# Meta columns and tokens in one operand: matmul passes of 264, 264 and 512 columns instead of 16, 512 and 512

## The reference

```python
meta = jnp.broadcast_to(meta_tokens.astype(x.dtype)[None], (B, N_META, D_MODEL))   # N_META = 16
h = jnp.concatenate([meta, x], axis=1)
L = h.shape[1]                                                                      # 1040
...
xn = rms_norm_2(h, norm_mix_g[layer])
proj = jnp.einsum('bld,de->ble', xn, w_in[layer])
q, k, v, f_logit, b_gate, c_gate, u = jnp.split(proj, split_at, axis=-1)
log_f = jax.nn.log_sigmoid(f_logit.astype(jnp.float32) + b_f[layer].astype(jnp.float32))
...
y_attn = forgetting_attention(q.reshape(hs), k.reshape(hs), v.reshape(hs), log_f)
y_conv = b_gate * causal_depthwise_conv(c_gate * u, conv_w[layer].astype(u.dtype))
```

## Time and profile before

| | |
|---|---|
| Median of 3 runs | 2525.3 us (2525.23 to 2527.97) |
| Profiled execution | 2522.91 us, span 2521.0 us |
| Mean granted clock of PE | 0.919 |
| PE busy | 2194.3 us (87%), 9596 matmuls |
| DVE busy | 1117.7 us (44%) |
| POOL busy | 498.1 us (20%) |
| ACT busy | 413.5 us (16%) |
| Chain that ended last | PE 71%, DVE 23%, ACT 2% |
| of it, line 594 | 60% |

### The profile page before, as it was taken

How to read it: one execution, slowest core, us unless ns; L and a number is a source line. 1 busy time by engine, 2 the same in 40 slices (tenths; PEclk the granted TensorE clock), 3 DMA queues, 4 the chain that set the end, 5 groups by cost and what they waited for, 6 DMA issues and landing times.

```text
span 2521.0 us, 23118 instructions
## 1 busy us (share of the span) xinstructions
PE 2194.3 (87%) x9596; PEld 1734.7 (69%) x9596; DVE 1117.7 (44%) x1222; ACT 413.5 (16%) x591; POOL 498.1 (20%) x375
## 2 busy tenths in 40 slices
PE   6999989797878229789999868799899999999997
PEld 5787778576666117568787644457788888888886
DVE  4143542769999973451452134541422221222123
ACT  3001441310110032120010033330320011011001
POOL 2232002122211001111322120002222222222221
PEclk8999889799889659799999879999899999999998
DMA  4223002122222002132224132232223333323332
GB/s 147 83 92 100 1 19 92 48 77 75 67 71 71 17 0 76 58 114 77 76 77 127 36 68 60 60 97 92 75 92 93 99 93 98 100 92 100 93 100 100
DMA packets 53443, 196.23 MB, mean 78 GB/s; under 512 B 6993, under 2 KB 7249, under 8 KB 52865
## 3 DMA queue, kind: packets, MB, share of 16 engines
q1 hardware_dynamic: 30144, 113.56, 14.5%
q0 software_dynamic: 22320, 81.27, 10.8%
q10 hardware_dynamic: 912, 0.51, 0.1%
HBM read 172.02 MB, written 8.46 MB: 72 GB/s over the span
## 4 chain that ended last, share of the span: by engine, by line
PE 71%; DVE 23%; ACT 2%; issue 2%; DMA 1%; POOL 1%; SPq 0%; DVEq 0%; ACTq 0%; POOLq 0%
PE PS L594 60%; DVE PS L1446 12%; PE PS L825 2%; DVE SMALL L1583 1%; PE PS L757 1%; DVE XL L1259 1%; PE PS L671 1%; PE PS L697 1%; DVE X L1422 1%; DVE Y L1420 1%; PE PS L801 1%; PE PS L635 1%; PE PS L640 1%; PE PS L802 1%; DVE SSUM L1269 1%
## 5 line engine op out<-in xcount | busy, mean ns | idle before, releaser
L594 PE MATMUL PS<-XH,WH 128*128 128x512 f32 x1840 | 607.5, 412 | 93.0 <-DVE GATE L1284 19.7
L594 PE MATMUL PS<-XL,WH 128*128 128x512 f32 x1840 | 587.7, 402 | 0.0
L594 PE MATMUL PS<-XH,WL 128*128 128x512 f32 x1840 | 583.8, 399 | 0.0
L514 POOL TENSOR_TENSOR WL<-WRAW,WH 128x1024 fp32r<-128x1024 f32 x155 | 377.1, 2433 | 536.3 <-DMA WH<-weights 536.3
L594 PEld LDWEIGHTS PS<-XH,WH 128*128 128x128 f32 x1840 | 345.7, 196 | 171.1 <-issue 29.7
L594 PEld LDWEIGHTS PS<-XL,WH 128*128 128x128 f32 x1840 | 359.1, 195 | 78.8
L594 PEld LDWEIGHTS PS<-XH,WL 128*128 128x128 f32 x1840 | 357.3, 194 | 78.5
L511 POOL DMA_DIRECT2D WH<-weights x155 | 89.4, 577 | 1407.0 <-PE PS L594 1399.0
L1446 DVE SCALAR_TENSOR_TENSOR PS<-G,TAPW,PS 128x1024 f32<-128x1024 f32 x232 | 299.3, 1290 | 8.1
L1713 DVE TENSOR_TENSOR X<-X,PS 128x1024 f32<-128x1024 f32 x64 | 78.2, 1221 | 245.8 <-PE PS L594 245.8
L1703 DVE SCALAR_TENSOR_TENSOR TM<-PS,RB 128x1024 f32<-128x1024 f32 x32 | 39.1, 1225 | 270.4 <-PE PS L594 270.3
(11 more groups left out here) (224 smaller groups left out, 2095.5 us busy)
## 6 DMA issues: line engine op xcount, KB each, us to landing
WRAW<-weights SPq DMA_DIRECT2D x155, 512.0 KB, 3.5
WH<-weights POOLq DMA_DIRECT2D x155, 512.0 KB, 3.8
XTOK<-x SPq DMA_DIRECT2D x8, 512.0 KB, 7.5
x_kept<-X SPq DMA_DIRECT2D x2, 2048.0 KB, 11.8
QQ<-QH SPq DMA_DIRECT2D x16, 256.0 KB, 5.2
X<-x_kept SPq DMA_DIRECT2D x2, 2048.0 KB, 7.7
out<-OT SPq DMA_DIRECT2D x8, 512.0 KB, 2.6
KE<-KH SPq DMA_DIRECT2D x8, 260.0 KB
```

The lines of the kernel that those rows point to most:

```text
L514: g.tensor_tensor(WL[:, u, :], WRAW[:, u, :], WH[:, u, :].bitcast(F32), ALU.subtract)\
L594: m = nc.tensor.matmul(dst[:, a:b], w, v[:, a:b], start=first and n == 0, stop=last and n == 2)
```

## The change

The operand of the stage becomes one array of 1040 columns, XHM and XLM, with the meta columns in front. In the 17 chunks with meta columns, each product is now formed over columns 0 to 264 (MA, 16 meta and 248 tokens, into bank 4 or 5), 264 to 528 and 528 to 1040 (both into `slot`, at the place that these tokens had before). B and Q chunks read the same array behind its first 16 columns. DVE takes 264 columns from bank 4 or 5 and 776 from the slot (`take_long`), both times RBM, which is RB with 16 ones in front. The product of C and U is formed over 1040 columns at once. The sum of the norm moves from bank 4 to bank 6, for all norms. A memset for the ones is added to POOL's constants. Some arrays get other addresses.

```diff
+MA = (META + HALF) // 2
...
+        XHM = fixed("XHM", [P, KD, L], F32R)
+        XLM = fixed("XLM", [P, KD, L], F32R)
...
-        RB = fixed("RB", [P, S])
+        RBM = fixed("RBM", [P, L])
+        RB = RBM[:, META:]
...
+            const(g.memset(RBM[:, 0:META], 1.0))
...
                     if meta_dst is not None:
-                        three(meta_dst, *w, XMH[:, k, :], XML[:, k, :], k == 0, k == KD - 1, ((0, META),))
-                    m = three(slot(use), *w, XH[:, k, :], XL[:, k, :], k == 0, k == KD - 1)
+                        three(meta_dst, *w, XHM[:, k, 0:MA], XLM[:, k, 0:MA], k == 0, k == KD - 1, ((0, MA),))
+                        m = three(slot(use), *w, XHM[:, k, META:], XLM[:, k, META:], k == 0, k == KD - 1,
+                                  ((MA - META, HALF), (HALF, S)))
+                    elif sp == SP_IN2:
+                        m = three(slot(use), *w, XHM[:, k, META:], XLM[:, k, META:], k == 0, k == KD - 1)
+                    else:
+                        m = three(slot(use), *w, XH[:, k, :], XL[:, k, :], k == 0, k == KD - 1)
...
-                    m = nc.tensor.matmul(bank(4)[0:8, P:2 * P], COLSEL[:, 7 - b:15 - b], src[:, b * P:(b + 1) * P],
+                    m = nc.tensor.matmul(bank(6)[0:8, 0:P], COLSEL[:, 7 - b:15 - b], src[:, b * P:(b + 1) * P],
...
-            def take_meta(c, dst, factor=None, rows=P):
-
-                src = bank(4 + c % 2)[0:rows, 0:META]
-                dve.wait_ge(psum_full, USE0 + c + 1)
-                if factor is None:
-                    then(v.tensor_copy(dst, src))
-                else:
-                    then(v.tensor_tensor(dst, src, factor, ALU.mult))
+            def take_long(c, dst, rows=P):
+
+                use = USE0 + c
+                dve.wait_ge(psum_full, use + 1)
+                then(v.tensor_tensor(dst[:, 0:MA], bank(4 + c % 2)[0:rows, 0:MA], RBM[0:rows, 0:MA], ALU.mult))
+                v.tensor_tensor(dst[:, MA:], slot(use)[0:rows, MA - META:], RBM[0:rows, MA:],
+                                ALU.mult).then_inc(evacuated, 1)
+                dve.wait_ge(evacuated, use + 1)
...
-                take_meta(w, T2[0][:, 0:META])
-                take(w, T2[0][:, META:])
-                take_meta(w + 1, CU[:, c, 0:META], T2[0][:, 0:META])
-                take(w + 1, CU[:, c, META:])
-                then(v.tensor_tensor(CU[:, c, META:], CU[:, c, META:], T2[0][:, META:], ALU.mult))
+                take_long(w, T2[0][:])
+                take_long(w + 1, CU[:, c, :])
+                then(v.tensor_tensor(CU[:, c, :], CU[:, c, :], T2[0][:], ALU.mult))
```

More of the change, by code:

```diff
@@ L114, in build @@
         o_xh = top[0]
-        XH = fixed("XH", [P, KD, S], F32R)
-        o_xl = top[0]
-        XL = fixed("XL", [P, KD, S], F32R)
+        o_xl = o_xh + KD * S * 4
+        XH = at("XH", [P, KD, S], o_xh, F32R)
+        XL = at("XL", [P, KD, S], o_xl, F32R)
+        XHM = fixed("XHM", [P, KD, L], F32R)
+        XLM = fixed("XLM", [P, KD, L], F32R)
         WRAW = fixed("WRAW", [P, 2, D])
@@ L142, in build @@
         area = top[0]
-        assert area + 76416 + 256 <= nc.sbuf_usable_end, (area, nc.sbuf_usable_end)
+        assert area + 75904 <= nc.sbuf_usable_end, (area, nc.sbuf_usable_end)
         XTOK = at("XTOK", [P, NB, D], area)
@@ L163, in build @@
         TAPW = at("TAPW", [P, KD, TAPS], area + 74688)
-        ONES = at("ONES", [P, P], area + 75680)
+        ONES = at("ONES", [P, P], o_xh + 65536)
         SQ1 = at("SQ1", [P, 2, S], o_xl + 16384)
@@ L179, in build @@
         QH2 = at("QH2", [P, S], area + 71232, F32R)
-        MXH = at("MXH", [8, P], area + 75328, F32R)
-        MXL = at("MXL", [8, P], area + 75840, F32R)
+        MXH = at("MXH", [8, P], o_rt, F32R)
+        MXL = at("MXL", [8, P], o_rt + 512, F32R)
         XMT = at("XMT", [META, D], area + 40960)
@@ L616, in one @@
                 def one(c, i):
-                    chunk(c, i, sp, bank(4 + c % 2)[:, 0:META] if meta else None)
+                    chunk(c, i, sp, bank(4 + c % 2)[:, 0:MA] if meta else None)
                 if norm_n is not None:
@@ L964, in _ @@
             heads_conv(0)
-            chunk(C_IN2 + I_F, None, SP_IN2, bank(4 + I_F % 2)[:, 0:META])
+            chunk(C_IN2 + I_F, None, SP_IN2, bank(4 + I_F % 2)[:, 0:MA])
             heads_conv(1)
@@ L973, in _ @@
                 c = C_IN2 + I_V + n
-                chunk(c, None, SP_IN2, bank(4 + c % 2)[:, 0:META])
+                chunk(c, None, SP_IN2, bank(4 + c % 2)[:, 0:MA])
                 for t in range(4 * n, 4 * n + 4):
@@ L994, in _ @@
                 act.dma_start(t[:], src).then_inc(small_in, 16)
-            act.wait_ge(consts, 8)
+            act.wait_ge(consts, 9)
             act.wait_ge(small_in, 16 * 6)
@@ L1000, in hi @@
                 scale = 1.0 if gain is None else GAINS[:, gain, k:k + 1]
-                nc.scalar.activation(XH[:, k, :], src, ACT.Copy, scale=scale).then_inc(x_hi, 1)
+                dst = XHM[:, k, META:] if sp == SP_IN2 else XH[:, k, :]
+                nc.scalar.activation(dst, src, ACT.Copy, scale=scale).then_inc(x_hi, 1)
             def square(n, k, src, sq=SQ):
@@ L1011, in norm @@
                 act.wait_ge(n_sum, n + 1)
-                nc.scalar.activation(RT[:], bank(4)[0:8, P:2 * P], ACT.Sqrt, scale=1.0 / D,
+                nc.scalar.activation(RT[:], bank(6)[0:8, 0:P], ACT.Sqrt, scale=1.0 / D,
                                      bias=EPS[0:8, 0:1] if NORM_EPS[n] == EPS_A else EPS[0:8, 1:2]).then_inc(n_root, 1)
@@ L1100, in meta_rms @@
                 for k in range(KD):
-                    ins = nc.scalar.activation(XMH[:, k, :], bank(5)[:, k * META:(k + 1) * META], ACT.Copy,
+                    ins = nc.scalar.activation(XHM[:, k, 0:META], bank(5)[:, k * META:(k + 1) * META], ACT.Copy,
                                                scale=GAINS[:, G_MIX, k:k + 1])
@@ L1254, in lo @@
                 dve.wait_ge(x_hi, KD * sp + k + 1)
-                h = XH[:, k, :].bitcast(F32)
+                h, l = XH[:, k, :].bitcast(F32), XL[:, k, :]
+                if sp == SP_IN2:
+                    h, l = XHM[:, k, META:].bitcast(F32), XLM[:, k, META:]
                 if gain is None:
-                    ins = v.tensor_tensor(XL[:, k, :], src, h, ALU.subtract)
+                    ins = v.tensor_tensor(l, src, h, ALU.subtract)
                 else:
-                    ins = v.scalar_tensor_tensor(out=XL[:, k, :], in0=src, scalar=GAINS[:, gain, k:k + 1], in1=h,
+                    ins = v.scalar_tensor_tensor(out=l, in0=src, scalar=GAINS[:, gain, k:k + 1], in1=h,
                                                  op0=ALU.mult, op1=ALU.subtract)
@@ L1325, in _ @@
             dve.wait_ge(evacuated, USE0 + GB0)
-            dve.wait_ge(consts, 33)
+            dve.wait_ge(consts, 34)
             for c in range(4):
@@ L1502, in meta_operand @@
                 for k in range(KD):
-                    ins = v.scalar_tensor_tensor(out=XML[:, k, :], in0=bank(5)[:, k * META:(k + 1) * META],
-                                                 scalar=GAINS[:, G_MIX, k:k + 1], in1=XMH[:, k, :].bitcast(F32),
+                    ins = v.scalar_tensor_tensor(out=XLM[:, k, 0:META], in0=bank(5)[:, k * META:(k + 1) * META],
+                                                 scalar=GAINS[:, G_MIX, k:k + 1], in1=XHM[:, k, 0:META].bitcast(F32),
                                                  op0=ALU.mult, op1=ALU.subtract)
@@ L1537, in _ @@
             w = C_IN2 + I_F
[L1538 to L1541, removed]
+            take_long(w, T2[0][0:8, :], 8)
             v.tensor_scalar(T2[0][0:8, :], T2[0][0:8, :], BF[:], None, ALU.add).then_inc(f_in, 1)
@@ L1563, in _ @@
                 w = C_IN2 + I_K + c
-                take_meta(w, K2[:, c, 0:META])
-                take(w, K2[:, c, META:])
+                take_long(w, K2[:, c, :])
                 if c < 3:
@@ L1602, in _ @@
                     dve.wait_ge(cum_kept, 32)
-                take_meta(w, VF[:, c, 0:META])
-                take(w, VF[:, c, META:])
+                take_long(w, VF[:, c, :])
                 for t in range(4 * c, 4 * c + 4):
```

6 lines of the change are left out of this document (2 added, 4 removed).

## The result

The changed kernel takes 2484.93 us (median of 4 runs, 2482.69 to 2497.58), against 2525.77 us (4 runs, 2525.23 to 2527.97) of the kernel before beside it: a ratio of 0.9847, 95% interval [0.9813, 0.9881]. It was run twice more, on other chips, beside some of the experiments, with ratios of 0.9863 [0.9838, 0.9887] and 0.9853 [0.9825, 0.988]. The forecast of 2487.3 us and its range held.

A forecast was written before the change was run, and what follows sets the result against it. PE bounds the kernel, busy 87% of the span, on the path almost everywhere in this stage. 36.2 + 0.8 + 1.1 - 0.1 = 38.0 us off 2525.3 gives 2487.3 us; step bounds 2483.4 to 2491.7, range 2482 to 2497.

The forecast's parts named there:

- The step: PE's work on one of 8 contraction slices in meta-column chunks: 1.7175 to 1.415 us, 120 steps behind the norm, 36.2 us.
- the upper end: Bound on the meta-column step: 512-column passes stay at 0.231 us, 264 costs 0.125; step 1.443, saving 0.274 us.
- The reason for the step: In meta-column steps, a 16-column pass costs the weight load beneath it, 0.11 us, not its columns.
- The cold stretches: Meta-column pieces behind the norm: about 22 us at 1.2 GHz lose 10.0 instead of 10.8 us, gain 0.8 us.
- Before the norm: Ten steps of the first two chunks: 3.0 us saved less 1.9 for a cold clock, gain 1.1 us (0 to 3.0).
- The layer-1 stretch: First layer-1 chunk, same DVE pace: clock stayed at 0.50 for 4.2 us after waiting ended; model for the 1.9 us loss.
- The last bound: Before the norm, PE sums squares that DVE has ready at 1097.78, so at most 3.3 us can be had.
- DVE: Takes of meta-column chunks stay at 1.40 us as 264 + 776 columns; at most 0.1 us lost on the path.
- Weights: POOL's next weight load takes 6.4 us against a chunk of 11.3 us: free, unless a load takes 5 us longer.
- The rival of another limit: Late weight loads or K's buffers freed late in the stage eat half of the 36 us: 2505 us; chance 0.08.
- The rest: 0: Outside the stage: a memset at the start of some 0.1 to 0.2 us, norm sums in another bank, other layers 0.
- The range's lower bound: Whole kernel, best case: 120 x 0.317 + 0.8 + 3.0 = 41.9 us gained, 2483.4 us.

The follow-up runs named there:

- the half load: Kernel before, its 16-column passes loading only 64 of 128 weight columns (half the meta features left out): 2510.53 us, ratio 0.9941.
- the spread passes: Kernel before, each 16-column pass placed directly ahead of the two 512-column passes of its own product: 2528.14 us, ratio 1.001.

## Why the prediction was right, point by point

- **The step.** Forecast 1.415, measured 1.42: 120 x (1.7175 - 1.42) = 35.7 us instead of 36.2. The price of the 264-column pass, taken from the 272-column rows of the attention, was 0.122 and is 0.12. A 512-column pass takes 0.231 in these steps, the upper end, and not 0.227, and that is the difference; the B chunks over the same array have it too. The 0.231 that the prediction worked out for the kernel before is what its trace has: four wide passes of a meta step take from 1093.16 to 1094.08, 0.230 each, where a B chunk has 0.227. So the wide passes were slower in a meta step before the change and after it, and the sum should have gone by 0.231. Why they are is open.

```profile
1093.16 0.63 PE L594 MATMUL PS<-XL,WH 128*128 128x512 f32 x2
1093.63 0.62 PE L594 MATMUL PS<-XH,WL 128*128 128x512 f32 x2
1094.08 0.17 PE L594 MATMUL PS<-XMH,WH 128*128 128x16 f32 x1
```

- **The reason for the step.** "A pass that narrow costs what sits beneath it, the weight load" holds, and the half load and the spread passes refined it: it is the next pass's load. For a row of three the sum is the same, which is why the prediction could not tell the two. The section of the Trainium skill that the prediction cites (TensorE: Matmul & The Clock Gate, Back-to-back issue gap) is no rule against the change: it gives N/2.4 + 2.5 ns for an isolated pass and says itself that at small widths this under-counts, because the weight load is not in it. The 0.11 us here agree with that.
- **The cold stretches.** Forecast a gain of 0.8 us, measured 2.5: the meta pieces behind the norm sum to 178.7 us against 120 x 1.42 = 170.4, so 8.3 us are lost instead of 10.8. The cold step was right, 2.6 us (6 passes at 0.22 and 3 at 0.43; these two rows are the same place in two steps, at clock 0.50):

```profile
1106.37 0.85 PE L597 MATMUL PS<-XHM,WH 128*128 128x264 f32 x2
...
1108.97 0.85 PE L597 MATMUL PS<-XHM,WH 128*128 128x264 f32 x2
```

  From 1106.37 to 1108.97 is 2.60. Mis-sized was the time spent cold, which was held at 22 us: 8.3 us at a loss of 1 - 1.42/2.60 = 0.454 each is 18. Most of it is at the last three V chunks, where 7.1 us of loss became 5.1. The granted clock says the same: it was at 0.50 for 4.0, 6.0 and 4.2 us from the start of these pieces before, and for 3.4, 4.1 and 2.7 us now. Why it came back sooner there is open.
- **Before the norm.** Forecast 1.1 us, measured 2.97. This is the step that failed. I had the clock stay low while PE waits, and for 4.2 us after. The windows (length, PE busy, then the other engines, then the granted clock) answer to the earlier trace rows:

```profile
1061.90:1073.30 11.40, 9.41 (x31) 7.29 (x30) 11.26 (x11) 3.45 (x3) 0.00 (x0) 0.50 0.00 0
1073.30:1083.60 10.30, 8.24 (x28) 6.12 (x28) 10.21 (x9) 4.14 (x4) 0.00 (x0) 0.53 0.00 0
1079.60:1082.90 3.30, 2.68 (x9) 1.97 (x9) 3.27 (x3) 1.15 (x2) 0.00 (x0) 0.50 0.00 0
1082.90:1086.30 3.40, 3.33 (x22) 3.08 (x23) 2.52 (x3) 2.11 (x4) 0.00 (x0) 0.99 0.02 5
1083.60:1090.00 6.40, 6.40 (x42) 5.80 (x42) 4.46 (x5) 4.51 (x6) 0.57 (x1) 1.00 0.29 84
```

  The first half held: before, the clock rose at 1073 while PE still waited, and now it stays at 0.50 to the end of the waiting. The second half did not: it rose right there, at 1082.9, and the ten steps begin at 1082.97. They took 14.47 us where ten warm ones take 14.2, an excess of 0.27; before, at full clock, they took 17.44 where ten take 17.18, an excess of 0.26. So none of the 1.9 us that the prediction took off for the clock was lost. The layer-1 stretch was a poor model for this, and why the clock came back later there is open. The last bound also held: SSUM is ready at 1087.18 + 9.89 = 1097.07 and PE ends at 1097.44, so nothing more can be had here.

```profile
1087.18 9.89 DVE L1280 TENSOR_TENSOR SSUM<-SSUM,SQ 128x1024 f32<-128x1024 f32 x6 [1.12 <-ACT SQ L1017]
```

- **DVE.** Forecast 0.43 + 0.97 us for a take, measured to the same digits, against 1.40 before; idle time ahead of these takes remains:

```profile
L1527 DVE TENSOR_TENSOR CU<-PS,RBM 128x776 f32<-128x776 f32 x4 | 3.9, 966 | 0.1
...
L1526 DVE TENSOR_TENSOR CU<-PS,RBM 128x264 f32<-128x264 f32 x4 | 1.7, 432 | 29.8 <-PE PS L597 29.8
```

- **Weights.** No wait of PE for WL stands in the chain of the stage: free, as said. The rival of another limit did not come.
- **"The rest: 0."** This was wrong in two places. "Some arrays get other addresses" was in my own account of the change, and I gave it no price. It cost 3.8 us in the feed-forward part (shown by the experiments) and 2.0 us in B and Q, whose cause is open. "Other layers are the same" failed in the part with the attention too, which gained 1.6 us and in later profiles 4 us.
- **The sum.** 35.7 + 2.5 + 2.97 = 41.2 us of gain in the stage against a forecast of 38.1, less 2.0 in B and Q, makes the 39.2 of the pieces. With 0.7 from the earlier start and 0.2 lost between the pieces these are the 39.7 at the end of the stage. Then come 1.6 from the part with the attention, -3.8 from the feed-forward part and -1.2 from the last: 36.3, as the span shows. That the forecast of 38.0 came so near is luck in part: an underestimate of 3.1 in the stage stood against an omission of 5.8. (The range's lower bound adds up to 41.7 and not 41.9 us of gain, which changes nothing.)

## What to carry to other kernels

Where every matmul loads its own weights, a pass costs no less than the load of the pass after it (0.11 us for 128 columns of weights), so a narrow remainder should not get a pass of its own: split the total evenly, so that the narrowest pass is as long as a load, and keep the count of passes. Where a change moves arrays, compare the distance between each matmul's moving operand and its weights before and after, by its remainder modulo 256 bytes; here two arrays that had nothing to do with the edit were moved by 64 bytes, which cost a tenth of the gain. Read the parts that the change does not touch as well. When a forecast comes out, add up its terms all the same: here two errors had cancelled.

## What the runs showed of the hardware that was not expected

- In float32r, 512-column passes follow at 226.7 ns where columns and weights lie a multiple of 256 bytes apart, at 227.5 to 230.5 ns (229 in the mean, by product) at 64 bytes beyond it, and at 233.3 ns at 128. This is for stretches of 512-column passes alone, in the feed-forward part; a remainder of 192 was not tried there.
- A 16-column pass with a 128-column load costs 0.11 to 0.12 us in a row and by itself; with a 64-column load behind it 0.06. Widths of 16 and 128 columns cost the same.
- The two levels of the clock: with waits between its steps PE stayed at 1.2 GHz for as long as the waits lasted, from 1061.9 to 1082.9, and was at 2.4 GHz from there on, where the last wait ended; in layer 1, behind the same kind of waits, it stayed at 1.2 GHz for 4.2 us more.
